# Exchanging rotated rows of queries and keys by partition shuffles on VectorE

## What is computed

```python
def apply_partial_rope(t, cos, sin):
    half = ROPE_DIM // 2                      # 8
    r1 = t[..., :half]
    r2 = t[..., half:ROPE_DIM]
    rot = jnp.concatenate([r1 * cos - r2 * sin, r2 * cos + r1 * sin], axis=-1)
    return jnp.concatenate([rot, t[..., ROPE_DIM:]], axis=-1)

dq = apply_partial_rope(da_q.reshape(B, S, 4, 2, 64), cos, sin)
dk = apply_partial_rope(da_k.reshape(B, S, 4, 2, 64), cos, sin)
...
s = jnp.einsum('bhmqd,bhmkd->bhmqk', qb, k) * scale
a = jax.nn.softmax(jnp.where(allowed, s, neg), axis=-1)
a = a[:, :, 0] - lam * a[:, :, 1]
return jnp.einsum('bhqk,bhkd->bhqd', a, v)
```

## Time and profile before

| | us |
|---|---|
| median of 3 runs | 2525.43 (2521.73, 2525.43, 2525.5) |
| span of the profiled execution | 2525.1 |
| TensorE (PE) busy | 2315.6 (92%) |
| VectorE (DVE) busy | 1001.0 (40%) |
| ScalarE (ACT) busy | 585.6 (23%) |
| GpSimd (POOL) busy | 410.2 (16%) |
| mean granted TensorE clock | 0.968 of full speed |

### The profile page before, as it was taken

The page is one execution under the profiler, slowest core; times in us unless marked ns, Lnnn a source line. Parts: engine busy times, 40 slices in busy tenths (PEclk is TensorE's granted clock), DMA queues, the critical chain, the costliest instruction groups (busy, mean ns, idle before and its releaser), DMA issues. The chain is left out here.

```text
span 2525.1 us, 29142 instructions
## 1 busy us (share of the span) xinstructions
PE 2315.6 (92%) x11776; PEld 1707.1 (68%) x11776; DVE 1001.0 (40%) x1730; ACT 585.6 (23%) x1211; POOL 410.2 (16%) x404
## 2 busy tenths in 40 slices
PE   7989999588889999999778988899999999999998
PEld 5766788444447766688644545787767887888886
DVE  5445533511135354543521114545653334322234
ACT  2433401211123352321301113423442001100011
POOL 2011121112211101111111211111111221111111
PEclk9999999799998999999989999899999999999999
DMA  4114535699982212232779995222322333233321
GB/s 147 51 44 102 133 106 203 235 410 415 415 332 67 67 34 61 64 89 89 305 306 416 415 398 190 68 84 68 88 76 71 93 103 101 84 99 94 100 92 67
DMA packets 291540, 402.85 MB, mean 160 GB/s; under 512 B 31306, under 2 KB 230730, under 8 KB 273478
## 3 DMA queue, kind: packets, MB, share of 16 engines
q1 hardware_dynamic: 276444, 373.31, 42.0%
q0 software_dynamic: 10176, 16.81, 1.8%
q10 hardware_dynamic: 4778, 10.76, 1.6%
HBM read 388.99 MB, written 30.15 MB: 166 GB/s over the span
## 5 line engine op out<-in xcount | busy, mean ns | idle before, releaser
L137 PE MATMUL banks<-h_split,w_high 128*128 128x512 f32 x2624 | 829.4, 397 | 2.7 <-PEq L3035 1.7
L137 PEld LDWEIGHTS banks<-h_split,w_high 128*128 128x128 f32 x2624 | 481.5, 188 | 107.9 <-issue 8.2
L189 DVE TENSOR_TENSOR w_low<-w_raw,w_high 128x1024 fp32r<-128x1024 f32 (+1 forms) x264 | 316.9, 1201 | 526.6 <-POOL w_high L178 526.5
L178 POOL CAST w_high<-w_raw 128x1024 fp32r<-128x1024 f32 (+1 forms) x264 | 278.2, 1055 | 1475.1 <-PE banks L137 1352.2
L137 PE MATMUL banks<-h_split,w_low 128*128 128x512 f32 x1312 | 514.6, 392 | 0.0
L137 PEld LDWEIGHTS banks<-h_split,w_low 128*128 128x128 f32 x1312 | 246.5, 188 | 55.0
L137 PE MATMUL banks<-w_high,op_split 128*128 128x512 f32 x736 | 231.3, 394 | 1.0 <-DVE mg_part L1269 1.0
L1839 PE MATMUL banks<-expert_ring,ex_xsT 128*64 128x256 f32 x1472 | 180.2, 400 | 17.3 <-DMA expert_ring<-in_w_exp_up 14.3
L137 PEld LDWEIGHTS banks<-w_high,op_split 128*128 128x128 f32 x736 | 138.2, 188 | 34.0 <-DVE mg_part L1269 2.2
L1839 PEld LDWEIGHTS banks<-expert_ring,ex_xsT 128*64 128x64 f32 x1472 | 107.5, 144 | 75.7 <-DMA expert_ring<-in_w_exp_up 15.5
L137 PE MATMUL banks<-w_low,op_split 128*128 128x512 f32 x368 | 144.7, 393 | 0.0
(11 more groups left out here) (424 smaller groups left out, 2768.6 us busy)
## 6 DMA issues: line engine op xcount, KB each, us to landing
w_raw<-in_w_in SPq DMA_DIRECT2D x142, 512.0 KB, 4.1
expert_ring<-in_w_exp_gate SPq DMA_DIRECT2D x46, 1024.0 KB
expert_ring<-in_w_exp_up SPq DMA_DIRECT2D x46, 1024.0 KB
expert_ring<-in_w_exp_down SPq DMA_DIRECT2D x46, 1024.0 KB
w_raw<-in_w_gu SPq DMA_DIRECT2D x44, 512.0 KB, 4.1
region<-in_w_exp_gate SPq DMA_DIRECT2D x20, 1024.0 KB
region<-in_w_exp_up SPq DMA_DIRECT2D x20, 1024.0 KB
region<-in_w_exp_down SPq DMA_DIRECT2D x20, 1024.0 KB
```

What stands on the lines that cost most here:

```text
L137: last = nc.tensor.matmul(out, left, right, start=(start and n == 0), stop=(stop and n == 2), skip_group_check=True)
L178: self.nc.gpsimd.tensor_copy(self.high[:, i % self.SPLIT, 0:n], self.raw[:, i % self.RAW, 0:n]).then_inc(self.high_ready, 1)
L189: self.nc.vector.tensor_tensor(self.low[:, i % self.SPLIT, 0:n], self.raw[:, i % self.RAW, 0:n], self.high[:, i % self.SPLIT, 0:n].bitcast ...
```

## The change

The permutation matrix, its load and the two `swap` matmuls of a head go. DVE instead shuffles partitions within each group of 32 (`stream_shuffle`, with the list `ROPE_PAIRS`: rows 0 to 7 and 8 to 15 exchanged, 16 to 31 in place) from the raw tile into the destination tile in SBUF, waits for it, multiplies in place by the sine and adds the cosine part. The sign that the matrix held goes into the table of frequencies, so that the sine's first 8 rows are negative. In the steady state, queries are rotated in step 1, after `split_low`, and keys in step 2. The order at the start is cosine, shuffle, sine, sum for queries, then for keys. The thresholds of the waits follow; banks 5 and 7 are no longer written by the rotation, so the wait for `y_out` moves to the projection of later heads.

```diff
+ROPE_PAIRS = [*range(8, 16), *range(8), *range(16, 32)]
-        self.rope_swap = sb("rope_swap", [P, P])
-        (raw[:, 3, :], t["c_neg_before"]),
-        (k.rope_swap[:], t["c_rope_swap"])]))
+        (raw[:, 3, :], t["c_neg_before"])]))
-            sp.wait_ge(start.landed[0], 16 * 7)
+            sp.wait_ge(start.landed[0], 16 * 6)
-            pool.wait_ge(start.landed[0], 16 * 7)
+            pool.wait_ge(start.landed[0], 16 * 6)
...
         def project(head, part, bank):
             for n, c in part:
                 if c == 0 and head > 1:
-                    pe.wait_ge(sem["rope_step"], 4 * (head - 1) + 3 + n)
+                    pe.wait_ge(sem["rope_step"], 4 * (head - 1) + 2 + 2 * n)
+                    if n == 0 and head > 2:
+                        pe.wait_ge(sem["y_out"], head - 2)
                 st.columns(pe, columns_of(head, n), c, bank)
-
-        def swap(head, n, bank):
-            if head:
-                pe.wait_ge(sem["raw_ready"], 2 * head + n - 1)
-            nc.tensor.matmul(k.ps[:, bank, :], k.rope_swap[:], raw[:, n, :], start=True,
-                             stop=True).then_inc(sem["swapped"], 1)
...
-        swap(0, 0, 0)
-        swap(0, 1, 1)
...
                 if t == 2:
-                    if head:
-                        pe.wait_ge(sem["y_out"], head)
-                    swap(head + 1, 0, 5)
-                    swap(head + 1, 1, 7)
                     fill(1)
...
-        def sin_part(head, n, bank):
+        def sin_part(head, n):
             dst = (qT, kT)[n][:, head % 2, :]
+            nc.vector.stream_shuffle(dst, raw[:, n, :], ROPE_PAIRS).then_inc(sem["swapped"], 1)
             dve.wait_ge(sem["swapped"], 2 * head + n + 1)
-            nc.vector.tensor_tensor(dst, k.ps[:, bank, :], sinT[:], ALU.mult).then_inc(sem["rope_step"], 1)
-            dve.wait_ge(sem["rope_step"], 4 * head + 3 + n)
+            nc.vector.tensor_tensor(dst, dst, sinT[:], ALU.mult).then_inc(sem["rope_step"], 1)
+            dve.wait_ge(sem["rope_step"], 4 * head + 2 + 2 * n)
             nc.vector.tensor_tensor(dst, dst, turned_part[:, n, :], ALU.add).then_inc(sem["qk_ready"], 1)
...
         for n in (0, 1):
             cos_part(0, n)
-        for n in (0, 1):
-            sin_part(0, n, n)
+            sin_part(0, n)
...
             if head + 1 < heads:
-                if t == 2:
-                    cos_part(head + 1, 0)
-                    cos_part(head + 1, 1)
-                    sin_part(head + 1, 0, 5)
-                    sin_part(head + 1, 1, 7)
                 if t in (1, 3):
                     st.split_low(dve, 21 + 3 * head + t // 2)
+                if t in (1, 2):
+                    cos_part(head + 1, t - 1)
+                    sin_part(head + 1, t - 1)
...
-            swap[head + half + i, head + i] = -1
-            swap[head + i, head + half + i] = 1
-            freq[head + i] = freq[head + half + i] = inv[i]
+            freq[head + i], freq[head + half + i] = -inv[i], inv[i]
```

More of the change, by code:

```diff
@@ L3286, in constants @@
     half = 8
-    swap = np.zeros((P, P), f)
     freq = np.zeros((P, 1), f)
@@ L3334, in constants @@
         "c_chunk_bias": np.where((r[:, None] < 64) & (r[None, :] >= 64), f(NEG), f(0)),
-        "c_rope_swap": swap,
         "c_rope_freq": freq,
```

## The result

The change made the kernel slower: **2532.51 us** (median of 5 runs, 2530.75 to 2533.83) against 2523.78 for the kernel before (5 runs on the same chip, 2521.73 to 2525.5). The ratio is 1.0035, 95% interval 1.0023 to 1.0047. The forecast was 2525.1 with a range up to 2529.8; the result lies outside it, in the case of slower, which had 12%. The profiled execution took 2533.83 us, with a span of 2532.1, 7.0 above the span before.

What follows compares the result with a forecast made beforehand. TensorE and DVE were taken to arrive together at the transposes, so saved matmul time becomes waits. Terms -0.6 + 3.5 - 3.2 = -0.3 us on the 2525.1 span give 2524.8; the median, 0.3 higher, is 2525.1, range 2521.0 to 2529.8.

Steps and rivals of the forecast that it cites:

- case of slower: Whole kernel: slower by more than about 5 us, from a long shuffle, a lower clock or something overlooked; 12%.
- Rival 3: Attention stages: TensorE's waits let the clock fall to 1.2 GHz at six places, +18 us, 2543; 3%.
- Step 2, nothing back: Between scores and transposes, six times: the 1.71 us of a swap pair becomes TensorE waiting for DVE's difference; no gain.
- Step 1: Queries' rotation before the maxima: hidden in head 0, 0.88 us late in heads 1 and 2; 3.5 us lost in all.
- overrun: Heads 1 and 2 of both layers: DVE's maxima start 0.88 us late behind the queries' rotation, and TensorE waits as long.
- Step 3 a little: Next head's scores, six times: a wait of 0.10 us for the keys' sum goes; 0.6 us gained.
- The shuffle's price: DVE's shuffle: 0.69 us plus 0.10 for loading the list, so 0.10 beyond an ordinary operation.
- The sine out of SBUF: DVE's sine products, now read from SBUF: no gain, by the trace's row, against the skill's 65 ns shorter.
- The starts: Start of each of the two stages: scores come 1.6 us earlier without the swaps; 3.2 us gained in all.
- The opening, nothing: Kernel's opening: one load less gains nothing, since DVE ends later than POOL's casts; otherwise worth under 0.5 us.
- Rival 1: Between scores and transposes: they don't wait for DVE, so TensorE's whole 13.7 us is saved, 2511.7; 6%.
- Rival 2: DVE's shuffle runs by groups of 32 partitions, 1.83 us beyond an ordinary operation; 17.5 us lost, 2542.9; 7%.

Runs made afterwards that it cites:

- swaps_cut_short: The kernel before, with the swaps of heads 1 to 3 cut from 512 columns to 8, no shuffle and no move: 2524.9 us, ratio 1.0002.
- start_only: The kernel before, with the shuffle for head 0 of a layer alone, heads 1 to 3 keeping the swaps: 2521.71 us, ratio 0.9986.
- idle_filled: The changed kernel, with two fp32 matmuls of 512 columns, results unread, put back per head where the swaps stood in step 2: 2524.34 us, ratio 1.0003.

## Why the prediction was wrong

**The step that failed is the clock.** The sum had it at nothing: step 2 turned the swaps' time into waits and left the work behind them at full speed. Rival 3 had the mechanism, the places (head 0 with 1.8 us of waiting, heads 1 and 2 with 2.6) and the level of 1.2 GHz, and got 3%. The chance was read off one row, a clock of 1.00 beside a wait of 1.74, but the waits forecast in four of six places, 2.6, were far longer than any that this row speaks for. It bore head 0 out (1.62, mostly no fall) and said nothing of 2.50, where 12 of 12 fell. The forecast carried the price of an idle engine as its idle time alone. The rival's size was wrong as well: it took some 3 us more at each of six places, 18 in all; a fall added 1.40 to 1.58, five of them 7.6. The prediction's last sign of being wrong, a clock under 1.00 in these stages, is what came.

The other steps, against the runs:

- *Step 2, nothing back*: held, as idle time. Transposes 209.72 - 206.92 = 2.80 after the scores in head 0, forecast 2.80; 3.68 in head 1, forecast 3.7. `swaps_cut_short` shows the same with no shuffle.
- *Step 1*: held. The overrun of 0.88 measured 0.90 at the maxima and 0.88 at the transposes.
- *Step 3 a little*: failed, by 0.6 us. From the last ordinary matmul to the scores it is still 0.33 (213.34 to 213.67), though the keys' sum now ends at 212.40. The 0.33 was the distance of these two kinds of matmul and no wait of 0.10.
- *The shuffle's price*: 0.73 and 0.01 for the list, within 0.05 of 0.69 + 0.10. The queries' rotation holds DVE for 236.80 - 234.03 = 2.77, forecast 2.74. The Trainium skill (VectorE: DVE Perf Modes, the perf-mode tier table) gave 0.70 as an estimate; the trace agrees within 5%.
- *The sine out of SBUF*: no gain, as the row said. It takes 0.69 for keys and 0.75 for queries (medians), with 0.68 out of PSUM before. By the Trainium skill (VectorE: DVE Perf Modes, the TRN2 errata) it would have been 65 ns shorter (an estimate), and the trace disagrees. Beside a cast on POOL it took up to 1.43, which no term of the sum had.
- *The starts*: 7.48 to 5.78 in the first layer (1.70, forecast 1.6), 1.2 in the second, for the slow sine product of 1.43. `start_only` has 2.6 for both, forecast 3.2.
- *The opening, nothing*: the first instruction of the stage came at 166.45, before at 165.95. The changed kernel's two other profiles have it at 165.83 and 165.28, so this 0.5 lies within what one execution differs from the next.
- *Rival 1*, the saving stays: excluded by the waits and the time. *Rival 2*, the long shuffle: excluded by its 0.73.
- *The range*: its upper end follows from the terms (2525.43 + 4.3). Its lower end of 2521.0 doesn't: with -1.9 the terms give 2523.5, and 3.7 under the forecast is 2521.4. Nothing hangs on it.

The changed kernel's own terms without the clock, -2.9 from the starts and +3.5 from the overruns, are close to a draw, and `idle_filled` measured that draw (1.0003). With four or five falls of 1.57 they make +6.9 to +8.5; the medians differ by 8.7.

## What to carry to other kernels

Matmuls taken off a TensorE that stands before a wait are not merely worth nothing: the hole they leave can lower the clock of the work behind it, which here cost 1.4 to 1.6 us for each wait of 2.5. When such work goes, pull other work from behind the wait into its place in the same edit (7.3 us under the kernel before, here). A row that shows the clock holding beside a wait speaks for that place: it says nothing of longer waits, and here waits of 1.17 and 1.62 elsewhere sometimes had a fall although one of 1.74 had none. On the engine that feeds the wait, put added work in front of its own idle time and not in front of what the other engine waits for.

## What was not expected of the hardware

- A fall followed each of twelve waits of 2.50 us, and 3 of 18 waits of 1.62; yet 2 of 6 waits of 1.17 in `swaps_cut_short`, and none of 26 waits of 1.68 at the stages' starts. The length alone doesn't decide.
- Matmuls that do nothing but keep TensorE busy can make a kernel faster: 10 us of them, put where TensorE would have waited, gained 8.
- A sine product of DVE with both inputs in SBUF took 1.43 us beside a cast on POOL and 0.69 without one; a product with one input in PSUM took 0.68 beside such a cast. Moving an operand from PSUM to SBUF can so make an operation slower, though not by itself.
- Loading the list of a shuffle takes 11 to 15 ns on DVE, and a shuffle of 128 x 512 in fp32 0.73 us, 0.04 more than a sum of that size. The changed kernel's queries, all eight times:

```profile
L1050 DVE LOAD_MASK_SELECT da_qT<-da_raw x8: 11/14/15, 167.1 to 1061.6; - x8
L1050 DVE STREAM_SHUFFLE da_qT<-da_raw x8: 729/731/752, 167.1 to 1061.6; 128x512 f32<-128x512 f32 x8
```
